# A lane gather moved three blocks back, two products moved behind a gate, and a latent attention made one step deeper

## The reference

```python
def swiglu(h, w13, w2):
    a, b = jnp.split(h @ w13, 2, axis=-1)
    return (jax.nn.silu(a) * b) @ w2

mod = c_act @ mod_w[i] + mod_b[i]          # 2 layers x 9 x 1024 columns, for modulate() and the gates
h = modulate(rmsnorm(x, norm_g[i, 0]), sh1, sc1)
x = x + FFN_RES * g1[:, None, :] * swiglu(h, ffn_w13[i, 0], ffn_w2[i, 0])

def attend(args):                          # 16 heads, q and k 96 wide, v 64 wide, blocks of 128 queries
    s = (einsum("bqhd,bkhd->bhqk", qn, k_nope) + einsum("bqhd,bkd->bhqk", qr, k_rope)) * scale
    s = jnp.where(k_idx[None, :] <= q_idx[:, None], s, -jnp.inf)
    p = jax.nn.softmax(s, axis=-1).astype(v.dtype)
    return jnp.einsum("bhqk,bkhd->bqhd", p, v)
return o @ w_o
```

## Time and profile before

| what | value |
|---|---|
| median of 3 runs | 1790.75 us (1790.13 to 1793.82) |
| the profiled execution: own time | 1790.15 us |
| its span in the trace | 1788.3 us |
| PE busy | 1702.4 us (95%) |
| DVE busy | 1261.5 us (71%) |
| ACT busy | 914.5 us (51%) |
| feed-forward calls 0, 1, 2 | about 50 to 246, 400 to 604, 609 to 807 us |
| heads of the latent attention | about 872 to 951 us |

### The profile page before, as it was taken

The page is one execution under the profiler, slowest core; times in us unless marked ns, Lnnn a source line. Parts: engine busy times, 40 slices in busy tenths (PEclk is TensorE's granted clock), DMA queues, the critical chain, the costliest instruction groups (busy, mean ns, idle before and its releaser), DMA issues.

```text
span 1788.3 us, 32986 instructions
## 1 busy us (share of the span) xinstructions
PE 1702.4 (95%) x11940; PEld 1558.6 (87%) x11940; DVE 1261.5 (71%) x2077; ACT 914.5 (51%) x1587; POOL 87.9 (5%) x151
## 2 busy tenths in 40 slices
PE   6999999999999999999989999999999999999998
PEld 5899988888999889998778999899877788989997
DVE  6888878768888888866556555689787465555554
ACT  1544457644444444444665444545377755554443
POOL 2000011200000000000001000100000000000000
PEclk9999999999999999999999999999999999999999
DMA  9888957757889788874334666354532155436651
GB/s 358 308 291 303 269 188 201 156 212 261 290 305 259 258 292 303 299 199 142 118 95 122 208 186 188 108 177 148 165 95 77 48 188 164 144 130 199 182 187 65
DMA packets 123656, 352.77 MB, mean 197 GB/s; under 512 B 9850, under 2 KB 52874, under 8 KB 114224
## 3 DMA queue, kind: packets, MB, share of 16 engines
q1 hardware_dynamic: 108128, 262.18, 45.3%
q10 hardware_dynamic: 12432, 78.65, 14.0%
q0 software_dynamic: 3008, 10.74, 1.8%
HBM read 347.31 MB, written 4.22 MB: 197 GB/s over the span
## 4 chain that ended last, share of the span: by engine, by line
PE 62%; DVE 17%; issue 9%; ACT 7%; DMA 2%; ACTq 1%; POOL 1%; DVEq 0%; POOLq 0%
PE ps L827 52%; DVE arena L356 4%; DVE w_lo L193 3%; ACT w_hi L1105 2%; ACT w_hi L187 2%; DMA arena<-in_mod_w 1%; DVE w_lo L1116 1%; PE ps L2942 1%; PE ps L3028 1%; DVE act_s L1145 1%; DVE arena L2635 1%; ACTq L330 1%; DVE resid L1269 1%; DVE arena L372 1%; PE ps L695 1%
## 5 line engine op out<-in xcount | busy, mean ns | idle before, releaser
L827 PE MATMUL ps<-t_hi,w_hi 128*128 128x256 f32 (+1 forms) x2616 | 751.4, 287 | 13.0 <-DVE t_lo L756 5.7
L827 PE MATMUL ps<-t_hi,w_lo 128*128 128x256 f32 (+1 forms) x2616 | 740.8, 283 | 1.3 <-issue 1.3
L827 PE MATMUL ps<-t_lo,w_hi 128*128 128x256 f32 (+1 forms) x2616 | 740.9, 283 | 0.0
L827 PEld LDWEIGHTS ps<-t_hi,w_hi 128*128 128x128 f32 (+1 forms) x2616 | 500.4, 191 | 30.4 <-issue 15.9
L827 PEld LDWEIGHTS ps<-t_lo,w_hi 128*128 128x128 f32 (+1 forms) x2616 | 500.6, 191 | 2.3
L827 PEld LDWEIGHTS ps<-t_hi,w_lo 128*128 128x128 f32 (+1 forms) x2616 | 500.5, 191 | 0.2
L1116 DVE TENSOR_TENSOR w_lo<-raw,w_hi 128x1024 fp32r<-128x1024 f32 x258 | 315.5, 1223 | 116.3 <-ACT w_hi L1105 116.3
L193 DVE TENSOR_TENSOR w_lo<-raw,w_hi 128x1024 fp32r<-128x1024 f32 x240 | 289.4, 1225 | 121.0 <-ACT w_hi L187 120.8
L1105 ACT ACTIVATE w_hi<-raw 128x1024 fp32r<-128x1024 f32 x258 | 268.9, 1053 | 163.0 <-PE ps L827 122.9
L187 ACT ACTIVATE w_hi<-raw 128x1024 fp32r<-128x1024 f32 x240 | 248.4, 1053 | 144.4 <-PE ps L827 101.7
L827 PE MATMUL ps<-w_hi,g_hi 128*128 128x512 f32 x440 | 174.9, 397 | 8.5 <-DVE g_lo L1148 8.5
(11 more groups left out here) (359 smaller groups left out, 1678.7 us busy)
## 6 DMA issues: line engine op xcount, KB each, us to landing
raw<-in_stream SPq DMA_DIRECT2D x498, 512.0 KB, 4.5
arena<-in_mod_w ACTq DMA_DIRECT2D x72, 1024.0 KB, 7.0
grow<-gate_scratch POOLq DMA_DIRECT2D x6, 512.0 KB, 8.1
u_scratch<-u_keep ACTq DMA_DIRECT2D x1, 3072.0 KB, 36.6
arena<-u_scratch POOLq DMA_DIRECT2D x8, 256.0 KB, 3.7
small<-in_small POOLq DMA_DIRECT2D x1, 1368.0 KB, 10.4
resid<-in_x POOLq DMA_DIRECT2D x1, 1024.0 KB, 18.6
arena<-in_mem POOLq DMA_DIRECT2D x1, 1024.0 KB, 5.4
```

The costliest lines, as they stand in the source:

```text
L827: last = TE.matmul(out, lhs, rhs, start=start and i == 0, stop=stop and i == 2)
```

## The change

Three edits. First, in `ffn`, `mod_gather` goes from behind block 0 to behind block 3 of the next body, and ACT's `mod_take` from behind the first split to behind both tiles, in front of the splits of blocks 4 and 5. Second, in the closing body with a chunk (calls 0 and 1), products 4 and 5 go from in front of the lo of block 2 to behind the last `g_lo`. Third, in the attention the weights are scaled by 1/sum before they are transposed (new `weigh`, three rotating buffers), the transposes come at step h+3, and values are computed for two heads at once and feature-major (`pair_values`: four matmuls with 64 stationary columns each, `tile_position` 0 or 64, 256 and 128 moving columns) into bank 7, from where `t_hi` and `t_lo` are split. `mix_tile` and `om` are gone; the loop has 20 steps.

```diff
-                        if owes is not None and j == 0:
+                        if owes is not None and j == 3:
                             mod_gather(pe, owes, turns)
...
             def act_body(act, i, static, mod, more, owes):
                 for t in range(2):
                     hi_next(act, i, 2 * t, static)
-                    if owes is not None and t == 0:
-                        mod_take(act, owes, turns)
                     act.wait_ge(used, h0 + 2 * t + 2 + RING * i)
...
                     hi_next(act, i, 2 * t + 1, static)
                     if mod is not None and more:
                         mod_load(act, t, mod + 1)
+                if owes is not None:
+                    mod_take(act, owes, turns)
                 if not (static and i == FG - 1):
                     hi_next(act, i, 4, static)
                     hi_next(act, i, 5, static)
...
+                    closing = t == 1 and static and i == FG - 1
-                    if mod is not None and not opening:
+                    if mod is not None and not opening and not closing:
                         mod_products(dve, mod, range(4 * t, 4 * t + 2), turns)
...
-                    if mod is not None and t == 1 and not opening and not (late_mod and static and i == FG - 1):
+                    if mod is not None and closing:
+                        mod_products(dve, mod, range(4 * t, 4 * t + 2), turns)
+                    elif mod is not None and t == 1 and not opening:
                         mod_products(dve, mod, range(4 * t + 2, 4 * t + 4), turns)
...
+        weights = (act_s[:, 0, 0:384], act_s[:, 1, 0:384], ar(10240, 384))
...
+        def weigh(h):
+            @block.vector
+            def _(dve):
+                dve.wait_ge(A.sem, summed[h])
+                VE.reciprocal(rinv, sums).then_inc(V.sem, V.up())
+                dve.wait_ge(V.sem, V.n)
+                for q, (lo, hi) in enumerate(((0, P), (P, 3 * P))):
+                    VE.tensor_scalar(sl[:, lo:hi], sl[:, lo:hi], rinv[:, q:q + 1], None, ALU.mult).then_inc(V.sem, V.up())
+            weighed[h] = V.n
...
+        def pair_values(j):
+            @block.tensor
+            def _(pe):
+                pe.wait_ge(A.sem, copied_p[2 * j + 1])
+                if j:
+                    pe.wait_ge(V.sem, mixed[j - 1])
+                for kt, (of, n) in enumerate(((0, L), (2 * P, P))):
+                    for odd in range(2):
+                        h = 2 * j + odd
+                        last = TE.matmul(ps[7][64 * odd:64 * odd + 64, L - n:L], vm[:, kt, h * 64:(h + 1) * 64], tmp[:, odd, of:of + n],
+                                         start=kt == 0, stop=kt == 1, tile_position=(0, 64 * odd))
+                last.then_inc(T.sem, T.up())
...
-        for step in range(HEADS + 3):
+        for step in range(HEADS + 4):
...
-            elif step < 18:
-                out_unit((step - 6) // 2, step % 2)
+            else:
+                out_unit((step - 6) // 2, step % 2, parts=(0,) if step == HEADS + 3 else (0, 1))
...
-            if step >= 5 and step % 2 == 1:
-                mix_tile((step - 5) // 2)
             if 0 <= step - 1 < HEADS:
                 scores(step - 1)
-            if 0 <= step - 2 < HEADS:
-                turn_weights(step - 2)
+            if step >= 5 and step % 2 == 1:
+                pair_values((step - 5) // 2)
+            if 0 <= step - 3 < HEADS:
+                turn_weights(step - 3)
...
-            if 0 <= step - 3:
-                values(step - 3)
+            if 0 <= step - 2 < HEADS:
+                weigh(step - 2)
```

More of the change, by code:

```diff
@@ L1933, in build @@
         vm = ar(8192, QT, D)
-        om = ar(10240, QT, D)
         latent = ar(10240, 4, 512)
@@ L2332, in scores @@
             scored[h] = T.n
+        weights = (act_s[:, 0, 0:384], act_s[:, 1, 0:384], ar(10240, 384))
+        summed = {}
         def softmax(h):
-            sl = act_s[:, h % 2, 0:384]
+            sl = weights[h % 3]
             nm, sums = st[:, 20 + 4 * (h % 2):22 + 4 * (h % 2)], st[:, 32 + 2 * (h % 4):34 + 2 * (h % 4)]
@@ L2370, in turn_weights @@
             copied_p[h] = A.n
[L2372 to L2385, removed]
-            @block.vector
-            def _(dve):
-                dve.wait_ge(A.sem, summed[h])
-                VE.reciprocal(rinv, sums).then_inc(V.sem, V.up())
-                dve.wait_ge(T.sem, at)
-                dve.wait_ge(V.sem, V.n)
-                for q in range(QT):
-                    VE.tensor_scalar(om[:, q, h * 64:(h + 1) * 64], ps[7][:, q * 64:(q + 1) * 64], rinv[:, q:q + 1], None,
-                                       ALU.mult).then_inc(V.sem, V.up())
-            kept_out[h] = V.n
-        def mix_tile(j):
+        def pair_values(j):
             slot = mixed_slot[j]
@@ L2402, in _ @@
             def _(pe):
-                pe.wait_ge(V.sem, max(kept_out.values()))
-                pe.wait_ge(A.sem, max(gathered.values()))
-                for q in range(QT):
-                    last = TE.transpose(ps[4][:, q * P:(q + 1) * P], om[:, q, j * P:(j + 1) * P], ident)
+                pe.wait_ge(A.sem, copied_p[2 * j + 1])
[6 more added lines that the diff above has]
+                                         start=kt == 0, stop=kt == 1, tile_position=(0, 64 * odd))
                 last.then_inc(T.sem, T.up())
-            at, done = T.n, blocks["pe"]
+            valued[j] = T.n
+            done = blocks["pe"]
             @block.scalar
             def _(act):
-                act.wait_ge(T.sem, at)
+                act.wait_ge(T.sem, valued[j])
                 act.wait_ge(used, done)
-                E.activation(t_hi[:, slot, :], ps[4][:, 0:L], ACT.Copy).then_inc(A.sem, A.up())
+                E.activation(t_hi[:, slot, :], ps[7][:, 0:L], ACT.Copy).then_inc(A.sem, A.up())
             hi_at = A.n
@@ L2419, in _ @@
                 dve.wait_ge(A.sem, hi_at)
-                VE.tensor_tensor(t_lo[:, slot, :], ps[4][:, 0:L], t_hi[:, slot, :].bitcast(F32), ALU.subtract).then_inc(V.sem, V.up())
+                VE.tensor_tensor(t_lo[:, slot, :], ps[7][:, 0:L], t_hi[:, slot, :].bitcast(F32), ALU.subtract).then_inc(V.sem, V.up())
             mixed[j] = V.n
@@ L2473, in build @@
                 next_split(lo_later=step == 18)
-        out_unit(6, 0)
-        mix_tile(7)
-        out_unit(6, 1)
+        out_unit(6, 1, parts=(1,))
         out_unit(7, 0)
```

12 lines of the change are left out of this document (7 added, 5 removed).

## The result

The changed kernel takes 1823.82 us (median of 4 runs, 1818.69 to 1825.17), the kernel before in the same session 1790.74: 1.0178 times as long, 95% interval 1.0163 to 1.0193. It is slower, as forecast, but by 33 us and not by 8, far outside the range. The profiled execution is the fastest of the four: own time 1818.69, span 1816.9, so 28.6 more than the span before.

A forecast was written before the change was run, and what follows sets the result against it. DVE and its round trips to ACT bound the loop bodies, PE the attention; +16.75 - 1.6 - 0.8 - 2.5 - 3.6 = +8.2 on 1790.15 gives 1798.4 us, 0.4% slower; 1791 to 1805 holds about 8 in 10.

The forecast's parts named there:

- the term: Loop bodies of calls 0 to 2: ACT's four moved copies add 0.67 in each of 25 bodies, +16.75 us.
- Rival 1: The copies hide in ACT's gap between DMA issue and split of block 4, so it is faster: 1782.5; chance 0.13.
- the step that let POOL go free: POOL's addition moves only behind the copies, with half a body until anything reads it; no cost in the sum.
- the ring: Loop bodies of calls 0 to 2: DVE's products release ACT, ACT's split releases DVE; nothing on it waits for PE.
- Edit 1's gain in call 1: Body 1 of call 1: without PE's stall at the gather, DVE's wait behind it goes, -1.6 us.
- the row of 1.59: Body 1 of call 1: the first gate's wait for the silu, and so for PE, taken as the gain there.
- The -0.8 of the weights' DMA: End of call 1's loop: DVE waits 0.82 for a weight DMA; a later DVE waits less, -0.8 us.
- Edit 2: Closing bodies of calls 0 and 1: two products behind the last gate, additions start earlier; -1.1 and -1.4, together -2.5 us.
- Edit 3: Attention: PE work -3.1, stalls removed -5.5, stalls added +5.0; together -3.6 us (-7.4 to +0.8).
- The rule that the prediction set against its row: Attention's added matmuls: tiles load and multiply in parallel, so a group costs about half of 1.51; sum some 3 us lower.
- the 5.0 taken for them: Attention: stalls added as `out_unit` closely follows its tile, 0.42 eight times is 3.4; taken as 5.0 (3.4 to 7).
- Rival 2: Body 1 of each call: PE's stall, moved to the down product, lowers the clock, 3 x 1.6, 1803 us; chance 0.10.

The follow-up runs named there:

- e2: Changed kernel with the four copies ahead of ACT's second DMA of mod weights, where ACT waits for DVE's products: 1808.74 us, ratio 1.0092 to the kernel before.
- e8: Changed kernel with the four matmuls of a pair of heads in the order of heads, not alternating between the column halves: 1821.48 us, one run.
- e10: Changed kernel with the odd head's values on the same column half as the even head's and summed with them: 1825.36 us, one run.
- e1: Changed kernel with the gate row of calls 0 and 1 written on POOL behind body 2 of the loop: 1805.4 us, ratio 1.0072 to the kernel before.
- e3: Changed kernel with copies ahead of ACT's second weights DMA and the gate row of calls 0 and 1 behind body 2: 1790.81 us, ratio 0.9991 to before.
- e5: e3 with the gate row of call 2 also behind body 2 of its loop: 1786.52 us, ratio 0.9983 to the kernel before.
- e11: e5 without edit 2, the last two products again ahead of the last gating: 1786.73 us, ratio 0.9981 to the kernel before.
- e4: Kernel before with edits 2 and 3 alone, the gather and its copies not moved: 1788.12 us, ratio 0.9980 to the kernel before.

## Why the prediction was right or wrong

**Right: the direction, and the mechanism that gave it.** DVE's products release ACT, ACT's split releases DVE, and the copies stand in between. Forecast were 0.67 a body, idle time of 1.26 and a period of 18.1; measured 0.72, 1.31 and 18.18. In calls 1 and 2 it was 0.79. The 19.1 us in 25 bodies are 2.3 above the term and within the bounds of 13.5 to 19.3. The 0.05 above the row in call 0: the copies took 0.70 here, with a gap of 0.03 behind them. Why calls 1 and 2 have 0.07 more was not traced. Rival 1 is dead: e2 shows that there is such a place, but in front of the DMA issue, not behind it.

**Wrong: the step that let POOL go free.** The prediction said: "POOL's addition moves too, but only behind the copies, with half a body until anything reads it". That looked at who reads what POOL writes, and not at what stands behind the addition in POOL's queue. There stand the gate row's product, a store that takes some 10 us to land, and a load. The sum put this at nothing. In the changed kernel's profile it cost 5.01 + 9.30 of waiting, and the norms behind the two waits lost 1.4 and 2.1 more, 17.8 us. In call 2 the first addition waited 0.6 longer than before (1.76 instead of 1.12, put down to PE). With the ring's 19.1 that makes 37.5. Against this stand 2.2 for body 1 of call 1, 2.6 in the two closing bodies, 1.1 of waits for the weights that are now covered, and 0.9 of waits for PE between the additions of call 1. That leaves 30.7, and the stages from call 0 to call 2 lost 10.2 + 1.4 + 10.9 + 8.1 = 30.6. The median has some 5 more than this execution; in e8 and e10 call 2 waits for the row as well. e1 took it away without touching the ring, e2 the ring without touching it, and e3 both. The trace of before would have given it: the load is issued 16 us ahead of its use and takes some 8 to land, so there were 8 us of slack, and the edit moves the copies by some 12 in a body of 17.5. A check of the slack of each queue behind a moved wait would have shown the excess.

**The terms that were mis-sized.** Edit 1's gain in call 1: forecast 1.6, measured 2.2; the row of 1.59 is the wait of the first gate alone. The -0.8 of the weights' DMA came: the wait of 0.82 is not in the changed kernel's profile. Edit 2: forecast 2.5, worth 1.7 (0.85 in each of two calls). The sum had 1.1 in call 0; in e5 DVE then waits 0.26 for the silu in front of the last gate, which the two products had covered. In call 1 the sum also had the products' wait of 0.30 for their DMA, and neither e5 nor e11 has that wait. In the changed kernel edit 2 only makes the wait for the row longer.

**Edit 3: the total right, its parts not.** Forecast -3.6, measured -4.1 in the changed kernel, in e4 and in e5. The group took 0.80 and not 1.1. The rule that the prediction set against its row (the Trainium skill, TensorEngine Tiling (Array Packing), Key Properties: different tiles load and multiply in parallel) agrees with e10, and the drain that the same list names would fit a side cost that the trace has: the scores in front of a group take 0.75 to the next start (926.03 to 926.78), in front of the transposes 0.65 (930.26 to 930.91). The stalls turned out smaller than the 5.0 taken for them:

```profile
L827 PE MATMUL ps<-w_hi,t_hi 128*128 128x512 f32 (+1 forms) x60 | 22.7, 379 | 3.3 <-DVE st L2366 1.4 <-DVE w_lo L193 0.9 <-DVE t_lo L2417 0.5
...
L2310 PE MATMUL ps<-cst,arena 128*96 128x128 f32 x64 | 9.7, 274 | 3.1 <-ACT arena L2318 3.0
```

This is the view of PE's lines in the changed attention (905 to 979): of the 3.3 at the products only 0.5 is the wait for `t_lo` of which the forecast was made, and prep still waits 3.0 for ACT's copies, which the forecast had as gone. Work of 8 x 0.80 in place of 11.9 and stalls of 6.4 against 7.8 before would give 6.9, so 2.8 us of added time in between are not traced to a row. That the 4.1 is near the 3.6 is in part luck.

**Rival 2, the moved stall and the clock.** The stall moved as described. PE's row of it in body 1 of call 0 answers to the earlier trace rows; DVE's first gate of body 1 in call 1, at 443.09, has no idle time now. Below the row, the windows behind the stall in calls 0, 1 and 2, all of the changed kernel:

```profile
84.13 0.80 PE L827 MATMUL ps<-w_hi,g_hi 128*128 128x512 f32 x1 [2.52 <-DVE g_lo L1149]
```

```profile
84.00:88.00 4.00, 3.87 (x11) 3.06 (x12) 2.65 (x5) 2.28 (x6) 0.20 (x1) 0.59 0.81 259
450.00:454.00 4.00, 3.95 (x22) 3.46 (x23) 2.58 (x4) 2.27 (x7) 0.20 (x1) 1.00 0.69 220
671.00:675.00 4.00, 3.15 (x15) 2.66 (x16) 2.98 (x4) 2.27 (x7) 0.07 (x1) 1.00 0.70 229
```

The clock fell once in three, and in the changed kernel this cost nothing that the rows show: the bodies behind the stall have the ring's period. Where the ring's price is gone, it does cost. In e2, e3, e5 and e11 the clock fell behind nine of the twelve moved stalls (2.45 to 2.56 us), and the body behind then took 17.91 to 18.17 from fold to fold; behind the other three (call 2 of e2, e3 and e11), where it stayed at 1.00, it took 17.46 or 17.47. So rival 2 is right about the mechanism, with 0.4 to 0.7 and not 1.6 a call, and in the changed kernel the ring hides it. In e5 all three calls have it, and call 0 is still not longer than before, as the closing body gives 0.85 back. The clock that did cost time in the changed kernel fell behind the wait for the gate row, a stall that the prediction did not have.

## What to carry to other kernels

When an edit moves a step to a later place, go through every queue that it releases, and for each ask what is queued behind the released instruction and how long before its use that lands. Here the four small copies were priced to within 0.12 us a body, and a DMA chain behind the third engine's wait, priced at nothing, cost about as much again. The slack is the time from issue to use less the transfer's own time: 16 us looked like enough for a move of 12, and 8 were not. Copies that must stand in a ring belong in front of the wait that the ring has anyway: the same four cost 0.72 to 0.79 a body behind that wait, and in front of it the body took 17.47 as before.

## What the runs showed of the hardware

Two matmul streams on the two column halves overlap, 0.80 against 1.45 for the same records on one half, whether they alternate or come one head after the other; that the order is without effect was not expected. And the granted clock does not follow the length of a stall alone: it fell to the lower level behind 5.9 and 10.2 us of idle time in front of a norm, and behind the moved stall, which is 2.45 to 2.56 us long everywhere, it fell in call 0 of the changed kernel and in all three calls of e5, and stayed at 1.00 in calls 1 and 2 of the changed kernel.
